# The output projections' input written slice by slice while the preceding projection runs: a two-layer trunk on one Trainium2 core

## What is computed

```python
# layer 0: causal pooling mixer (1024 channels) beside an mLSTM memory (4 heads of 256)
y_pool = pool_mix(buf, T, w_pool, pool_scale) * silu(z_p)
y_m = (hcell.reshape(B, T, M_W) * mh_norm_g) * silu(z_m)
y = einsum('bte,ed->btd', concatenate([y_pool, y_m], -1), w_out)
x = x + y
# layer 1: sparse attention, 16 heads in 4 groups, three branches combined by gates
o = gate[..., 0:1] * o_c + gate[..., 1:2] * o_s + gate[..., 2:3] * o_w
y = einsum('bte,ed->btd', o.reshape(B, T, NSA_W) * silu(z), w_out)
x = x + y
```

## Time and profile before

| | us |
|---|---|
| median of 3 runs | 2304.81 (2300.78 to 2307.51) |
| the profiled execution | 2303.34 |
| its span, first to last instruction | 2301.5 |
| PE busy | 2176.0 |
| DVE busy | 817.3 |
| ACT busy | 737.3 |
| POOL busy | 749.7 |
| mean granted clock of PE | 0.978 of full |

### The profile page before, as it was taken

One profiled execution on the slowest core, in us unless ns is written; L12 is line 12 of the kernel. 1 busy time (PEld: TensorE's weight loads), 2 busy tenths in 40 slices (PEclk: granted clock), 3 DMA queues, 4 the chain that ended last, 5 costly groups with the idle time before them and its releaser, 6 DMA issues.

```text
span 2301.5 us, 43763 instructions
## 1 busy us (share of the span) xinstructions
PE 2176.0 (95%) x17835; PEld 2046.8 (89%) x17835; DVE 817.3 (36%) x1724; ACT 737.3 (32%) x1029; POOL 749.7 (33%) x588
## 2 busy tenths in 40 slices
PE   3899999999999989978999999999999999998996
PEld 3899999999999989978888998889888988888995
DVE  6412204333150361123236521662245422653114
ACT  4322123323242342223334332443334332343221
POOL 1244433434434234442330242123321233113440
PEclk7999999999999999989999999999999999999998
DMA  6222363746456354453544344343534344423331
GB/s 229 74 80 79 107 212 92 206 129 170 138 123 189 107 129 114 114 176 93 144 113 120 104 117 130 82 130 101 157 92 124 102 130 115 114 62 111 113 103 78
DMA packets 453104, 282.00 MB, mean 123 GB/s; under 512 B 17112, under 2 KB 445720, under 8 KB 450611
## 3 DMA queue, kind: packets, MB, share of 16 engines
q1 hardware_dynamic: 452939, 279.68, 43.4%
HBM read 250.83 MB, written 45.99 MB: 129 GB/s over the span
## 4 chain that ended last, share of the span: by engine, by line
PE 58%; issue 22%; POOL 10%; DVE 7%; ACT 2%; POOLq 0%; DVEq 0%; ACTq 0%
PE ps L364 46%; POOL w_lo L342 10%; PE ps L1016 2%; PE ps L1109 1%; PE ps L931 1%; PE ps L952 1%; PE ps L1049 1%; PE ps L1113 1%; PE ps L1087 1%; ACT scratch L1323 1%; PE ps L1117 1%; DVE x_res L427 1%; DVE xy L1836 1%; DVE h_lo L424 0%; PE ps L942 0%
## 5 line engine op out<-in xcount | busy, mean ns | idle before, releaser
L342 POOL TENSOR_TENSOR w_lo<-w_raw,w_hi 128x512 fp32r<-128x512 f32 x584 | 749.5, 1315 | 1500.8 <-ACT w_hi L326 1174.8
L364 PE MATMUL ps<-h_hi,w_hi 128*128 128x260 f32 x4672 | 974.2, 290 | 56.5 <-DVE h_lo L424 34.6
L364 PE MATMUL ps<-h_hi,w_lo 128*128 128x260 f32 x4672 | 945.1, 284 | 0.0
L364 PE MATMUL ps<-h_lo,w_hi 128*128 128x260 f32 x4672 | 944.2, 284 | 0.0
L364 PEld LDWEIGHTS ps<-h_hi,w_hi 128*128 128x128 f32 x4672 | 727.9, 190 | 88.0 <-issue 60.4
L364 PEld LDWEIGHTS ps<-h_hi,w_lo 128*128 128x128 f32 x4672 | 724.3, 189 | 0.0
L364 PEld LDWEIGHTS ps<-h_lo,w_hi 128*128 128x128 f32 x4672 | 724.1, 190 | 0.0
L326 ACT ACTIVATE w_hi<-w_raw 128x2048 fp32r<-128x2048 f32 x134 | 256.9, 1917 | 26.4 <-DMA w_raw<-in_w_in 18.2
L460 DVE TENSOR_TENSOR xy<-ps,x_res 128x520 f32 x32 | 22.4, 700 | 281.6 <-PE ps L364 281.6
L472 ACT ACTIVATE scratch<-xy 128x520 f32 (+1 forms) x32 | 20.4, 639 | 280.9 <-DVE xy L460 280.9
L1323 ACT ACTIVATE scratch<-ps,scratch 128x128 f32<-128x128 f32 (+3 forms) x128 | 66.4, 524 | 134.4 <-DVE scratch L1728 133.9
(11 more groups left out here) (313 smaller groups left out, 1810.0 us busy)
## 6 DMA issues: line engine op xcount, KB each, us to landing
w_raw<-in_w_in SPq DMA_DIRECT2D x114, 1024.0 KB, 5.7
w_raw<-in_w_out SPq DMA_DIRECT2D x32, 1024.0 KB, 6.0
scratch<-in_cache_kv_sel SPq DMA_DIRECT2D x256, 64.0 KB, 1.9
scratch<-in_cache_kv_win SPq DMA_DIRECT2D x128, 128.0 KB, 2.5
scratch<-in_cache_kv_cmp SPq DMA_DIRECT2D x256, 64.0 KB, 2.0
out_kvw_s<-in_cache_kv_win SPq DMA_DIRECT2D x24, 512.0 KB, 6.9
x_scratch<-xy SPq DMA_DIRECT2D x2, 4160.0 KB, 14.3
x_res<-x_scratch SPq DMA_DIRECT2D x32, 260.0 KB, 6.0
```

The costliest lines, as they stand in the source:

```text
L342: ins = nc.gpsimd.tensor_tensor(WL[:, t.p, k:k + 4], WR[:, t.p, k:k + 4], WH[:, t.p, k:k + 4].bitcast(F32), ALU.subtract)
L364: mm = nc.tensor.matmul(PS[:, bank + c, 0:HALF], lhsT=w[:, t.p, k, :], rhs=h[:, k, c * HALF:(c + 1) * HALF], start=(k == 0 and x == 0), st ...
```

## The change

`project` can signal after each slice but the last (`tell`, semaphore `k_read`); it does so in the last input projection of either layer (tile 56, and tile 129, whose parts run in attention turns 12 to 15 of the last group). The split is cut into ranges of slices: `y_hi` on ACT waits per slice for that signal instead of for the whole projection, `y_lo` on DVE follows. In layer 0 slices 0 to 13 are split between the normalisation of slices 14 and 15 and their gating; ACT does so before tile 56's Silu and before the split of tile 58. In layer 1 slices 0 to 3, 4 to 8 and 9 to 11 are split in turns 12, 13 and 14, on DVE between `backed` and the sample sums. Slices 14 and 15 of layer 0 and 12 to 15 of layer 1 follow at the old places.

```diff
--- before.py
+++ after.py
@@ -343,7 +343,7 @@
                                               WH[:, t.p, k:k + 4].bitcast(F32), ALU.subtract)
             ins.then_inc(S["w_split"], 1)
 
-        def project(pe, t, h_need=None, part=(0, KT), bank=None, between=None):
+        def project(pe, t, h_need=None, part=(0, KT), bank=None, between=None, tell=False):
 
 
             if part[0] == 0:
@@ -364,6 +364,8 @@
                         mm = nc.tensor.matmul(PS[:, bank + c, 0:HALF], lhsT=w[:, t.p, k, :],
                                               rhs=h[:, k, c * HALF:(c + 1) * HALF],
                                               start=(k == 0 and x == 0), stop=(k == KT - 1 and x == 2))
+                if tell and k < KT - 1:
+                    mm.then_inc(S["k_read"], 1)
             if part[1] == KT:
                 mm.then_inc(S["proj_done"], 1)
 
@@ -435,16 +437,17 @@
                 act.wait_ge(S["h_tmp"], r * KT + k + 1)
                 nc.scalar.activation(HH[:, k], XR[:, k % 2], ACT.Copy).then_inc(S["h_hi"], 1); own.done("h_hi")
 
-        def y_split_act(act, own, r, done):
-
-            act.wait_ge(S["proj_done"], done)
-            for k in range(KT):
-                if r == 0 and k == 14:
-                    act.wait_ge(S["m_yz"], 10)
+        def y_hi(act, own, r, ks, done=None):
+
+            for k in ks:
+                if done is None:
+                    act.wait_ge(S["k_read"], (KT - 1) * r + k + 1)
+                elif k == ks[0]:
+                    act.wait_ge(S["proj_done"], done)
                 nc.scalar.activation(HH[:, k], XY[:, k], ACT.Copy).then_inc(S["y_hi"], 1); own.done("y_hi")
 
-        def y_split_dve(dve, own, r):
-            for k in range(KT):
+        def y_lo(dve, own, r, ks):
+            for k in ks:
                 dve.wait_ge(S["y_hi"], r * KT + k + 1)
                 nc.vector.tensor_tensor(HL[:, k], XY[:, k], HH[:, k].bitcast(F32), ALU.subtract
                                         ).then_inc(S["h_ready"], 1); own.done("h_ready")
@@ -887,7 +890,7 @@
                 for a in range(2):
                     mm = M(PS[:, 4 + a, 0:HALF], lhsT=ones, rhs=qT[:, 0, a * HALF:(a + 1) * HALF], start=True, stop=True)
                 mm.then_inc(S["m_ssq"], 1)
-                project(pe, Tile(M_BASE, 9, h, 10))
+                project(pe, Tile(M_BASE, 9, h, 10), tell=(h == 3))
                 pe.wait_ge(S["m_var"], h + 1)
 
 
@@ -1090,7 +1093,8 @@
                         scores(n + 1)
 
                     cuts = (4, 7, 10, 14, 16) if jj == 0 else (0, 4, 9, 14, 16)
-                    project(pe, Tile(A_BASE, 10 + jj, g, 14), part=(cuts[i], cuts[i + 1]), bank=2)
+                    project(pe, Tile(A_BASE, 10 + jj, g, 14), part=(cuts[i], cuts[i + 1]), bank=2,
+                            tell=(g == 3 and jj == 3))
                     if n == 0:
                         cmp_turn()
                     else:
@@ -1236,11 +1240,16 @@
                 A(RS[:], RS[:], ACT.Sqrt).then_inc(S["m_sqrt"], 1); own.done("m_sqrt")
                 t = Tile(M_BASE, 9, h, 10)
                 table(own, ACT.Silu)
+                if h == 3:
+                    act.wait_ge(S["m_yz"], 8)
+                    act.wait_ge(S["pl_y"], 9)
+                    y_hi(act, own, 0, range(KT - 2))
                 act.wait_ge(S["proj_done"], t.n + 1)
                 A(halves(S0["kT"][:, 1]), ps2(t), ACT.Silu).then_inc(proj_read[t.p], 1); act.wait_ge(proj_read[t.p], t.m + 1)
                 split_hi(act, own, t.ahead(2))
 
-            y_split_act(act, own, 0, O0_BASE)
+            act.wait_ge(S["m_yz"], 10)
+            y_hi(act, own, 0, range(KT - 2, KT), O0_BASE)
             out_act(act, own, 0, O0_BASE)
             act.wait_ge(proj_read[0], (G1_BASE + 1) // 2)
             act.wait_ge(proj_read[1], G1_BASE // 2)
@@ -1350,11 +1359,13 @@
 
                         split_half(act, own, Tile(A_BASE, 9 + (n + 3) // 4, g, 14).ahead(2) if n % 4 == 0 else
                                    Tile(A_BASE, 9 + (n + 2) // 4, g, 14).ahead(2), n % 4)
+                    if g == 3 and n >= 12:
+                        y_hi(act, own, 1, (range(0, 4), range(4, 9), range(9, 12), ())[n - 12])
                     if n == 15:
                         split_hi(act, own, Tile(A_BASE, 13, g, 14).ahead(2))
             act.wait_ge(S["a_ys"], 5)
             act.wait_ge(S["a_yz"], 16)
-            y_split_act(act, own, 1, O1_BASE)
+            y_hi(act, own, 1, range(12, KT), O1_BASE)
             out_act(act, own, 1, O1_BASE)
             act.wait_ge(proj_read[0], N_TILES // 2)
             act.wait_ge(proj_read[1], N_TILES // 2)
@@ -1590,6 +1601,8 @@
                     ins = STT(y, y, PR[:, bass.ds(R_MH + 2 * h + j, 1)], RS[:].rearrange("p (o t) -> p o t", o=1),
                               ALU.mult, ALU.mult)
                 step(ins)
+                if h == 3:
+                    y_lo(dve, own, 0, range(KT - 2))
                 t9 = Tile(M_BASE, 9, h, 10)
                 dve.wait_ge(proj_read[t9.p], t9.m + 1)
                 for j in range(2):
@@ -1598,8 +1611,7 @@
                 dve.wait_ge(S["st_out"], 32 * h + 32)
                 dve.wait_ge(S["n_out"], 16 * h + 16)
 
-            dve.wait_ge(S["m_yz"], 10)
-            y_split_dve(dve, own, 0)
+            y_lo(dve, own, 0, range(KT - 2, KT))
             out_dve(dve, own, 0, O0_BASE)
             dve.wait_ge(proj_read[0], (G1_BASE + 1) // 2)
             dve.wait_ge(proj_read[1], G1_BASE // 2)
@@ -1804,6 +1816,8 @@
                         CP(ptc, PS[0:64, 7, :]).then_inc(S["a_ptc"], 1); own.done("a_ptc")
                     else:
                         backed(n - 1)
+                    if g == 3 and n >= 12:
+                        y_lo(dve, own, 1, (range(0, 4), range(4, 9), range(9, 12), ())[n - 12])
                     if n == 14:
                         dve.wait_ge(S["d_own"], g + 1)
                         TT(on[:, 2], on[:, 2], PS[:, 4, 384:416], ALU.add).then_inc(S["d_vs"], 1); own.done("d_vs")
@@ -1827,7 +1841,7 @@
                 gated(3)
                 TT(XY[:, bass.ds(4 * g, 4), TP:TA], on[:, 2].rearrange("p (j b) -> p j b", b=NS), S1["zs"], ALU.mult
                    ).then_inc(S["a_ys"], 1); own.done("a_ys")
-            y_split_dve(dve, own, 1)
+            y_lo(dve, own, 1, range(12, KT))
             out_dve(dve, own, 1, O1_BASE)
             dve.wait_ge(proj_read[0], N_TILES // 2)
             dve.wait_ge(proj_read[1], N_TILES // 2)
```

## The result

The changed kernel takes 2309.05 us in the median (2306.14 to 2314.31), the one before 2304.38 (2300.78 to 2308.91), each over 17 runs: a ratio of 1.0021, with 1.0015 to 1.0027 as its 95% interval, or +4.7 us. The forecast was 2310.4, +5.6 us against before. So the two kernels differ by 0.2%, clear of the noise but small. The profiled execution has a span of 2308.7 us, 7.2 more than before. Of the 2.5 us over the median difference nearly all is the choice of executions: the profiled one before ran 1.0 us under its kernel's median, the one after (2310.45) 1.4 us over.

What follows compares the result with a forecast made beforehand. TensorE (PE), busy 95% of the span, was taken to bound the kernel. Layer 0's -0.9 us and layer 1's +6.5 us gave +5.6 us on a median of 2304.81: 2310.4 us, range 2303 to 2316.

Steps and rivals of the forecast that it cites:

- Layer 0, order of events: Layer 0's end: PE starts tile 57 without its wait, then waits for slices 12 and 14; -0.9 us.
- its bounds: Limits put on layer 0's forecast change: 0 and -3.1 us.
- Layer 1, turn 12: +3.0: Turn 13's transposes, last group: four subtractions ahead of DVE's sum make them 3.0 us later, no slack.
- Turn 13: +10.85: Turn 14's transposes, layer 1: five subtractions beside POOL (6.91 us), ahead of DVE's copy, make them 10.85 us later.
- 1.0 for the clock on the scores: Turn 14's scores, layer 1: low clock after the 3.0 us wait, between 0 and 1.5 us, taken as 1.0.
- Turn 14: +1.2: Turn 15's transposes, layer 1: three subtractions (2.2 us) ahead of a sum with 1.2 us to spare; 1.2 us later.
- 2.15 for the clock: Layer 1, after the 7.9 us wait before turn 14's transposes: half speed for 4.3 us, costing 2.15 us.
- Tile 130: Layer 1's first output tile: starts at 2086.8 at full clock, read at 2098.6 instead of 2092.1, +6.5 us.
- Rival 1: Low clock stays at the start of tile 130, losing 1.8 us: sum 7.4, 2312.2 us; chance 0.26.
- Rival 2: Both layers: each subtraction held for a whole POOL piece, pitch 1.95 instead of 1.69; 2313.2 us; chance 0.09.
- Rival 3: Added work fits DVE's idle time, both boundaries give their whole 18.0 us: 2286.8 us; chance 0.05.
- the boundary's most: Layer 1's output projection: the most the change can save, first tile read at 2083.4 instead of 2092.1, 8.7 us.

Runs made afterwards that it cites:

- The layer's part alone: Changed kernel with only layer 0's early split; layer 1 splits all 16 slices at the old place; 0.9999 of the kernel before.
- two slices: Changed kernel with two early layer 1 slices in each of turns 12 to 14, six instead of twelve; 0.9998 of the kernel before.
- layer 1's part alone: Changed kernel with only layer 1's early split; layer 0 splits all slices at the old place; 2314.42 us against 2306.46 before, ratio 1.0035.
- the idle slots: Changed kernel with ten early layer 1 subtractions, in twos, mostly where DVE stood idle, ACT's copies moved along; 2295.13 us against 2305.12 before, ratio 0.9958.

## Why the prediction was right

Measured +4.7 us (3.5 to 6.2 by the interval), forecast +5.6, with most of the chance on no change beyond 0.3%. The mechanism is the forecast one: DVE's subtractions ahead of the sum and the copy that PE's next turn waits for. In the pair of profiles, on which the steps can be compared, both layers came out some 0.7 us slower than forecast, while the medians differ by 0.9 us less than forecast. By its steps:

- *Layer 0, order of events.* Forecast: slice 14 at 841.25, read at 842.8 at full clock and 844.95 with the clock, -0.9. Measured: 841.38, read at 844.62, -1.27, then 1.0 lost in tile 58, which leaves -0.26: the low clock lasted 5.1 us behind slice 14's wait, not the 4.3 put down. The copies ended at 829.4 as forecast. The layer's part alone gave no difference that can be measured, which its bounds contained.
- *Layer 1, turn 12: +3.0.* Measured +2.9 (2052.31 against 2049.68, plus the 0.26 that the execution was ahead). No slack, as the earlier trace rows said; with two slices +1.43.
- *Turn 13: +10.85, and 1.0 for the clock on the scores.* Measured +12.3 with both. The subtractions took 6.68 (forecast 6.91), and the low clock more than was put down: the maxima came 1.5 us later than by turn 12's shift alone, and half speed in the projection let `backed` end at 2061.15, so that it, and no longer only the copy, held the first subtraction. With layer 1's part alone, where the clock was full there, it is +10.81: the work was forecast to 0.04 us, and the clock's term was 1.5 instead of 1.0. PE's wait was 6.42 us instead of the forecast 7.9 because half speed made it busy for longer first; at the full clock it was 7.71.
- *Turn 14: +1.2, and 2.15 for the clock.* Together 3.35, measured 3.31 at turn 15's transposes. With the rest the forecast was 15.2 at the last transpose, measured 15.65 against turn 12's start.
- *Tile 130.* Forecast at full clock with no wait in it, read 6.5 us later; measured 7.20 by L1, 6.94 with layer 0's 0.26 off. Rival 1 (low clock at its start) did not happen in this execution, where the low clock had ended at 2071.9. In the idle slots the clock did fall at that tile, with no wait of 6.9 us ahead of it, so the prediction's argument against this rival was not a safe one. And that both of layer 1's clock terms came out near their size in the profiled execution is in part luck: with layer 1's part alone the first of them was nothing.
- *Rival 2*, a full block behind each POOL piece, by which five would take 8.6 us: 6.68 to 6.97 in three executions. The Trainium skill, page "SBUF — State Buffer", section "Who interferes with whom", is borne out in that such subtractions contend with POOL; the exclusive lock, by which each waits out a whole piece, is not.
- *Rival 3*, that the work fits DVE's idle time, was wrong for the change's places; at other places most of ten slices did fit: in the idle slots L1 falls by 7.0 of the 8.7 us that the first paragraph gave as the boundary's most.

The two profiles differ by nothing but the boundaries: before the first (812.50 and 812.46), between them, and behind tile 130's read (209.4 and 209.6 us to the end) they agree to 0.2 us. Their stretches at 1.2 GHz sum to 100 us before and 104 after, and the difference lies at the boundary of layer 1. Other executions differ elsewhere as well: the 11 profiles have between 82 and 107 us at 1.2 GHz, and stretches near 75 and 1030 us, which no edit touches, are longer or shorter by 3.4 us or missing; 3.4 us of busy PE cost 1.7. That this makes the spread of the runs is argued from these profiles, not shown run by run.

## What to carry to other kernels

Before moving work into a busy stage, look on its engine at the instruction behind it and at the start of whoever waits for that: with 0.2 us between an end and a start, four subtractions of 2.90 us put ahead moved PE by 2.89, though DVE was busy for 36% of the span only. Twelve early subtractions there made layer 1's end 7.2 us longer; ten, in twos and for the most part where DVE had stood idle, made it 7.0 us shorter. The slots to use are those where the trace shows the engine waiting for the bound engine itself. And a wait that is removed or made should be priced twice, with the low clock beside it and without: from one profiled execution to another it came or stayed away.

## What was not expected of the hardware

- The same wait of 2.72 us ahead of turn 13's transposes stood in a stretch of 6.8 us at the 1.2 GHz level in the changed kernel (2051.4 to 2058.2, of which PE worked 5.7 from 2052.3 on) and with the clock at full in the run with layer 1's part alone. Where it was low, the 1.31 us that it cost the scores set back everything behind them.
- The clock can fall well before a long wait ends. Ahead of turn 14 it was low from 2065.1 to 2071.9, and only the last 3.1 us fell on work, as the wait lasted until 2068.72. So the longer wait was the cheaper one by the clock.
- Before the change the clock fell at 2071.85, 0.3 us into the wait of 6.9 us ahead of tile 130, so the length of that wait is not what brought it down. In the version in idle slots, where the wait is gone, it fell at much the same point (2067.94, 0.4 us into tile 130) and stayed low for 3.4 us; the only wait near was 1.67 us, in a turn in which PE was busy 5.0 of 6.7 us before the change. In the same version without layer 0's part it did not fall there.
